# Meta queries of a latent attention layer: scores as masked rows instead of small column products

## The chip, the cores and the metric

The kernel runs on one core of one Trainium2 chip. The metric is the device time of one execution in microseconds (us); lower is better. All arithmetic is fp32; the large products are made of three products each, of operands split into a rounded upper part (`_hi`) and a rest (`_lo`).

## The reference

Two transformer blocks of two layers each, 1024 wide, over 256 tokens; in the first block 16 meta tokens stand in front of them (272 positions, `T`). The change lies in the second layer of the first block, a latent attention with 16 heads:

```python
s = (jnp.einsum('bqhd,bkhd->bhqk', qn, k_nope)
     + jnp.einsum('bqhr,bkr->bhqk', qr, k_rope)).astype(jnp.float32) * scale
p = jax.nn.softmax(jnp.where(mask, s, -jnp.inf), axis=-1)
return jnp.einsum('bhqk,bkhd->bqhd', p.astype(v.dtype), v)
```

A query sees keys of its own chunk of 64 positions and of earlier ones; the 16 meta positions are the first chunk, so that a meta query sees the 16 meta keys only. Each head's query and key are 96 wide (64 without position, 32 rotary). What follows this layer is a feed-forward net with a causal convolution over three positions, and after it only the 256 real tokens count. So of the meta positions only the last two (14 and 15) are carried through this attention: 258 columns of queries instead of 272.

## The kernel before

The kernel is one program with an instruction list per engine: TensorE (PE) multiplies, VectorE (DVE) and ScalarE (ACT) move results out of PSUM, split weights into their two parts and do the softmax, GpSimd (POOL) does sums of squares and small copies, SyncE loads weights. Engines wait on semaphores. The order of the work is written out by hand.

The latent stage is `latent_stage` on each engine. PE goes over 32 weight blocks (step `s`, `latent_block`), and between them come the steps of eight pairs of heads `n`, at the steps given by `SCORES_AT["B"]`, `TURN_AT["B"]` and `MIX_AT["B"]`; steps over 31 lie between the first pieces of the output projection. For a pair:

- `latent_scores` (PE): for both heads `e` the scores of two query tiles of 128 against 144 and 272 keys (L1025). An fp32 product is two records in the trace.
- `latent_maxima` (DVE): four operations (L2271) that add the mask, write `S` and give the smallest value of the negated scores, then the bias for the exponential (`nb`, L2277).
- `latent_probs` (ACT): four exponentials (L1683). `latent_norm` (DVE): one over the sums, then four scalings (L2298).
- `latent_turn` (PE): the probabilities are transposed (L1037, L1041), after `normed`. `latent_pt` (ACT) copies them to `PT`.
- `latent_mix` (PE): the product with the values (L1055), after `b_meta_placed`.

The scores go to one of three banks, `score_bank(n, e)`; `maxed` counts the maxima and frees the banks.

The two meta queries of four heads are handled together, with the odd pair `n` of each two (group `b = n // 2`, four groups). In `latent_scores` there are four products (L1019, eight records) with 16 meta keys stationary and two query columns moving, which give keys down the rows and 8 columns. DVE negates and copies them (L2266), then after `nb` transposes a 32x32 block (L2283), takes the minimum (L2285) and makes the bias (L2287). ACT takes one exponential of 8x16 after the pair's four (L1688). `latent_norm` ends with the reciprocal (L2303), the scaling (L2306) and the transposition back (L2308). POOL then copies 16x8 into `PT` (L2725) and signals `b_meta_placed`, for which `latent_mix` of both pairs of the group waits. The semaphore `meta_dve` counts DVE's steps.

Two pieces run once: at step 1 DVE clears two tiles of 32x128 (L2154, L2155) after two rests of the latent products (L2231) and ahead of the split of the next weights (`refill`, L1956); at step 6 it lays out the meta positions' scale factors (`fm`, L2191), which PE transposes (L1000) and ACT stores as `rq`.

## Time and profile before

| | |
|---|---|
| median of 3 runs | 1211.8 us (1211.45 to 1211.91) |
| the profiled execution's own time | 1211.74 us |
| its span in the trace | 1209.9 us |
| latent stage's scores, turns and mixes | about 362 to 423 us of the span |
| PE clock granted | 1.00 throughout |

The span runs from the first to the last instruction in the trace; the execution's own time has 1.8 us more around it. The engines overlap, so that a busy time is no share of the end by itself. In a timeline each row has its start, the time from its start to the end of the last of its group, the engine, the line, the operation, output and inputs, and the count; idle time of the engine before it and what ended it stand in brackets. Matmuls overlap one another in the record, so what one costs is the distance from its start to the next one's.

### The profile page before, as it was taken

What the parts mean: (1) busy time and instruction counts of PE and PEld (TensorE: products, weight loads), DVE (VectorE), ACT (ScalarE), POOL (GpSimd) and SP (SyncE); (2) the same over time, 40 slices, a digit from 0 to 9 for tenths busy, and PEclk for the clock granted to TensorE, in tenths of its full rate; (3) what the DMA queues carried; (4) which work ended last, traced back from release to release, by engine and by line L of the source; (5) the groups of instructions that cost most, each with busy time, mean ns of one, the idle gap of its engine ahead of it and who ended that gap; (6) DMA issues with size and microseconds to landing.
All of it is one profiled execution on the core that took longest, in us unless ns stands there. A gap on an engine that the chain in (4) does not pass through costs nothing.

```text
span 1209.9 us, 26142 instructions
## 1 busy us (share of the span) xinstructions
PE 1202.5 (99%) x9943; PEld 1170.7 (97%) x9943; DVE 883.0 (73%) x1720; ACT 698.2 (58%) x1371; POOL 165.9 (14%) x176
## 2 busy tenths in 40 slices
PE   9999999999999999999999999999999999999998
PEld 8999999999998899999999999999999999999998
DVE  6988777776778878777668987666656877767443
ACT  6776555554468755554448855564336785556332
POOL 1111500002330040000670032000210003100000
PEclk9999999999999999999999999999999999999999
DMA  9333444435543245554566345455553334455451
GB/s 347 122 140 113 165 178 173 173 120 192 205 165 105 79 154 188 186 184 144 189 229 239 117 148 201 175 196 187 176 196 129 132 134 175 175 194 189 177 192 49
DMA packets 32237, 203.71 MB, mean 168 GB/s; under 512 B 3584, under 2 KB 4608, under 8 KB 11792
## 3 DMA queue, kind: packets, MB, share of 16 engines
q1 hardware_dynamic: 31248, 198.95, 45.9%
q0 software_dynamic: 896, 3.49, 0.8%
q8 instruction: 62, 1.02, 0.3%
q14 instruction: 31, 0.25, 0.1%
HBM read 201.10 MB, written 1.05 MB: 167 GB/s over the span
## 4 chain that ended last, share of the span: by engine, by line
PE 94%; DVE 4%; ACT 1%; issue 1%; DMA 0%; SPq 0%; ACTq 0%; DVEq 0%
PE ps L801 28%; PE ps L802 28%; PE ps L803 28%; DVE w_lo L1956 1%; PE ps L1209 1%; PE ps L902 1%; PE ps L903 1%; PE ps L904 1%; PE ps L1194 1%; PE ps L1180 1%; PE ps L1296 1%; PE ps L1055 1%; PE ps L1025 0%; DVE E_S L2411 0%; DMA raw<-in_weights 0%
## 5 line engine op out<-in xcount | busy, mean ns | idle before, releaser
L1956 DVE TENSOR_TENSOR w_lo<-raw,w_hi 128x1024 fp32r<-128x1024 f32 (+2 forms) x391 | 463.2, 1218 | 94.8 <-ACT w_hi L1429 93.9
L1429 ACT ACTIVATE w_hi<-raw 128x1024 fp32r<-128x1024 f32 (+2 forms) x391 | 376.0, 1002 | 188.9 <-PE ps L803 186.2
L801 PE MATMUL ps<-x_hi,w_hi 128*128 128x256 f32 (+2 forms) x1384 | 396.7, 287 | 0.1
L802 PE MATMUL ps<-x_lo,w_hi 128*128 128x256 f32 (+2 forms) x1384 | 392.0, 283 | 0.0
L803 PE MATMUL ps<-x_hi,w_lo 128*128 128x256 f32 (+2 forms) x1384 | 391.3, 283 | 0.0
L801 PEld LDWEIGHTS ps<-x_hi,w_hi 128*128 128x128 f32 x1384 | 260.6, 188 | 3.3 <-issue 1.6
L802 PEld LDWEIGHTS ps<-x_lo,w_hi 128*128 128x128 f32 x1384 | 260.3, 188 | 0.4
L803 PEld LDWEIGHTS ps<-x_hi,w_lo 128*128 128x128 f32 x1384 | 260.3, 188 | 0.0
L801 PE MATMUL ps<-X_x_hi,w_hi 128*128 128x256 f32 (+2 forms) x568 | 161.6, 285 | 0.0
L802 PE MATMUL ps<-X_x_lo,w_hi 128*128 128x256 f32 (+2 forms) x568 | 160.1, 282 | 0.0
L803 PE MATMUL ps<-X_x_hi,w_lo 128*128 128x256 f32 (+2 forms) x568 | 159.3, 281 | 0.0
L801 PE MATMUL ps<-G_g_hi,w_hi 128*128 128x256 f32 x512 | 143.8, 281 | 0.0
L802 PE MATMUL ps<-G_g_lo,w_hi 128*128 128x256 f32 x512 | 143.8, 281 | 0.0
L803 PE MATMUL ps<-G_g_hi,w_lo 128*128 128x256 f32 x512 | 143.8, 281 | 0.0
L801 PEld LDWEIGHTS ps<-X_x_hi,w_hi 128*128 128x128 f32 x568 | 106.8, 188 | 0.6 <-issue 0.5
L803 PEld LDWEIGHTS ps<-X_x_hi,w_lo 128*128 128x128 f32 x568 | 107.0, 188 | 0.0
L802 PEld LDWEIGHTS ps<-X_x_lo,w_hi 128*128 128x128 f32 x568 | 106.8, 188 | 0.1
L803 PE MATMUL ps<-F_g_hi,w_lo 128*128 128x272 f32 (+1 forms) x352 | 100.3, 285 | 0.0
L801 PE MATMUL ps<-F_g_hi,w_hi 128*128 128x272 f32 (+1 forms) x352 | 100.2, 285 | 0.0
L802 PE MATMUL ps<-F_g_lo,w_hi 128*128 128x272 f32 (+1 forms) x352 | 99.9, 284 | 0.0
L802 PEld LDWEIGHTS ps<-G_g_lo,w_hi 128*128 128x128 f32 x512 | 96.6, 189 | 0.0
L803 PEld LDWEIGHTS ps<-G_g_hi,w_lo 128*128 128x128 f32 x512 | 96.6, 189 | 0.0
(337 smaller groups left out, 1818.0 us busy)
## 6 DMA issues: line engine op xcount, KB each, us to landing
raw<-in_weights SPq DMA_DIRECT2D x159, 1024.0 KB, 4.8
raw<-in_weights SPq DMA_DIRECT2D x32, 704.0 KB, 4.1
raw<-in_weights SPq DMA_DIRECT2D x4, 832.0 KB, 4.4
E_bias<-in_even_bias POOLq DMA_DIRECT2D x4, 768.0 KB, 8.8
raw<-in_weights SPq DMA_DIRECT2D x6, 256.0 KB, 6.8
out<-h SPq DMA_DIRECT2D x8, 128.0 KB, 4.8
h<-in_tokens SPq DMA_DIRECT2D x3, 272.0 KB, 6.5
cst<-in_consts SPq DMA_DIRECT2D x1, 808.0 KB, 11.0
```

What stands on the lines that cost most here:

```text
L801: pe.matmul(target, hi, xs[0], start=start, stop=False)
L802: pe.matmul(target, hi, xs[1], start=False, stop=False)
L803: return pe.matmul(target, lo, xs[0], start=False, stop=stop)
L902: pe.matmul(to, x[0], w_hi[:, at + w0:at + w1], start=c == 0, stop=False)
L903: pe.matmul(to, x[0], w_lo[:, at + w0:at + w1], start=False, stop=False)
L904: mm = pe.matmul(to, x[1], w_hi[:, at + w0:at + w1], start=False, stop=c == KC - 1)
L1055: mm = pe.matmul(bank(7, to, cols, slice(64 * e, 64 * e + 64)), oB[v][0:keys, f:f + 64], oB["PT"][0:keys, at:at + cols], start=k == 0, sto ...
L1180: mm = pe.matmul(bank(3 + e, col, nk), a.o["qk"][p, q + t * P:q + t * P + P], a.o["qk"][p, k:k + nk], start=a.name == "E", stop=a.name == ...
L1194: tr = pe.transpose(bank(5 + e, b * P, P), a.o["S"][:, at + b * P:at + b * P + P], c_("ident", 0, P))
L1209: mm = pe.matmul(bank(7, n % 2 * SEQ + lo, cols, slice(64 * e, 64 * e + 64)), a.o["V"][:, vc:vc + 64], a.o["PT"][:, at:at + cols], start=k ...
L1429: act.activation(w_hi[:, to + a:to + b], raw[:, fr + a:fr + b], ACT.Copy).then_inc(hi_made, 1)
L1956: dve.tensor_tensor(w_lo[:, to + a:to + b], raw[:, fr + a:fr + b], w_hi[:, to + a:to + b].bitcast(F32), ALU.subtract).then_inc(lo_made, 1)
```

## The change

For a group of four heads the products are made the other way round. The four heads' queries at one meta position `c` are stationary (four columns, one from each head), and the 16 meta keys of all four heads move past them (64 columns). Two products, `c` = 0 and 1, write rows 0 to 3 and rows 32 to 35 of the bank. Of the 64 columns a row needs the 16 of its own head; a mask `mm` puts the rest out of play. DVE adds mask and negated scores and takes the minimum in one operation per `c`; ACT's exponential covers 64 rows by 64 columns; the scaled result goes to `mN` with 32 columns per head, is transposed as 64x128, and POOL places it with two copies, one per `c`. The factors `fm` are laid out for 64 rows. `meta_dve` counts four steps a group instead of six.

```diff
-                     ("rk", 8, F32), ("rq", 4, F32), ("nb", 32, F32), ("mS", P, F32), ("mT", P, F32), ("mP", P, F32),
-                     ("PTq", P, F32), ("mx", 16, F32), ("PT", 4 * B_TURNED, F32))
+                     ("rk", 8, F32), ("rq", 4, F32), ("nb", 32, F32), ("mT", 256, F32), ("mP", 256, F32), ("mN", 512, F32), ("mm", 64, F32),
+                     ("PTq", 528, F32), ("mx", 16, F32), ("PT", 4 * B_TURNED, F32))
...
+        def four_heads(name, n):
+
+            at = (n - 1) % 4 * 2 * T
+            return oB[name][:, at:at + 4 * T].rearrange("p (h t) -> p h t", h=4)
...
-                tr = pe.transpose(bank(6, 80, 16, slice(0, 32)), oB["fm"][0:16, 0:32], ident)
+                tr = pe.transpose(bank(6, 80, 16, slice(0, 64)), oB["fm"][0:16, :], ident)
...
-                    for e in range(2):
-                        for i in range(2):
-                            pe.matmul(bank(score_bank(n, 0), 416 + 4 * e + 2 * i, 2, slice(0, META)), stacked("K", n - 1 + i, e, 0, META),
-                                      stacked("Q", n - 1 + i, e, META - 2, 2), start=True, stop=True)
+                    keys, queries = four_heads("K", n), four_heads("Q", n)
+                    for c in range(2):
+                        pe.matmul(bank(score_bank(n, 0), 416, 64, slice(32 * c, 32 * c + 4)), queries[:, :, META - 2 + c],
+                                  keys[:, :, 0:META], start=True, stop=True)
...
-                    act.wait_ge(meta_dve, 1 + 6 * b + 3)
-                    act.activation(oB["mP"][0:8, 32 * b:32 * b + META], oB["mT"][0:8, 32 * b:32 * b + META], ACT.Exp,
+                    act.wait_ge(meta_dve, 1 + 4 * b + 1)
+                    act.activation(oB["mP"][0:64, 64 * b:64 * b + 64], oB["mT"][0:64, 64 * b:64 * b + 64], ACT.Exp,
...
-                        dve.memset(oB["mS"][0:32, :], 0.0)
-                        dve.memset(oB["mP"][0:32, :], 0.0).then_inc(meta_dve, 1)
+                        dve.memset(oB["mT"][0:64, :], 0.0)
+                        dve.memset(oB["mN"][0:64, :], 0.0)
+                        dve.memset(oB["mx"][0:64, :], 0.0)
+                        for c in range(2):
+                            rows, own = slice(32 * c, 32 * c + 32), CST["ident"] + 32 * c
+                            op = dve.tensor_scalar(oB["mm"][rows, :].rearrange("p (h k) -> p h k", h=4),
+                                                   cst[rows, own:own + 4].unsqueeze(2).broadcast_to([32, 4, META]), -NEG, NEG, ALU.mult, ALU.add)
+                        op.then_inc(meta_dve, 1)
...
-                    dve.tensor_scalar(oB["mS"][0:META, 32 * b:32 * b + 8], bank(score_bank(n, 0), 416, 8, slice(0, META)), -1.0, None, ALU.mult)\
-                       .then_inc(meta_scored, 1)
+                    for c in range(2):
+                        rows = slice(32 * c, 32 * c + 4)
+                        op = dve.tensor_tensor_reduce(oB["mT"][rows, 64 * b:64 * b + 64], bank(score_bank(n, 0), 416, 64, rows), oB["mm"][rows, :],
+                                                      -1.0, BIG, ALU.add, ALU.min, oB["mx"][rows, 4 * b:4 * b + 1])
+                    op.then_inc(meta_scored, 1)
...
-                    dve.transpose(oB["mT"][0:32, 32 * b:32 * b + 32], oB["mS"][0:32, 32 * b:32 * b + 32]).then_inc(meta_dve, 1)
-                    dve.wait_ge(meta_dve, 1 + 6 * b + 1)
-                    dve.tensor_reduce(oB["mx"][0:8, 4 * b:4 * b + 1], oB["mT"][0:8, 32 * b:32 * b + META], AX.X, ALU.min).then_inc(meta_dve, 1)
-                    dve.wait_ge(meta_dve, 1 + 6 * b + 2)
-                    dve.scalar_tensor_tensor(oB["mx"][0:8, 4 * b + 1:4 * b + 2], oB["mx"][0:8, 4 * b:4 * b + 1], -1.0, oB["rq"][0:8, 2:3],
+                    dve.scalar_tensor_tensor(oB["mx"][0:64, 4 * b + 1:4 * b + 2], oB["mx"][0:64, 4 * b:4 * b + 1], -1.0, oB["rq"][0:64, 2:3],
...
-                    part = oB["mP"][0:8, 32 * b:32 * b + META]
-                    dve.tensor_scalar(part, part, oB["mx"][0:8, 4 * b + 3:4 * b + 4], None, ALU.mult).then_inc(meta_dve, 1)
-                    dve.wait_ge(meta_dve, 1 + 6 * b + 5)
-                    dve.transpose(oB["PTq"][0:32, 32 * b:32 * b + 32], oB["mP"][0:32, 32 * b:32 * b + 32]).then_inc(meta_dve, 1)
+                    dve.tensor_scalar(oB["mN"][0:64, P * b:P * b + P].rearrange("p (h k) -> p h k", h=4)[:, :, 0:META],
+                                      oB["mP"][0:64, 64 * b:64 * b + 64].rearrange("p (h k) -> p h k", h=4),
+                                      oB["mx"][0:64, 4 * b + 3:4 * b + 4], None, ALU.mult).then_inc(meta_dve, 1)
+                    dve.wait_ge(meta_dve, 1 + 4 * b + 3)
+                    dve.transpose(oB["PTq"][0:64, P * b:P * b + P], oB["mN"][0:64, P * b:P * b + P]).then_inc(meta_dve, 1)
...
-                pool.tensor_copy(oB["PT"][0:META, :].rearrange("p (n e c) -> p n e c", n=2, e=2)[:, :, :, 0:2],
-                                 oB["PTq"][0:META, 32 * b:32 * b + 8].rearrange("p (e n c) -> p n e c", n=2, e=2)).then_inc(b_meta_placed, 1)
+                for c in range(2):
+                    own = oB["PTq"][32 * c:32 * c + META, P * b:P * b + 4 * 33].rearrange("p (h r) -> p h r", h=4)
+                    op = pool.tensor_copy(oB["PT"][0:META, :].rearrange("p (h r) -> p h r", h=4)[:, :, c:c + 1], own[:, :, 0:1])
+                op.then_inc(b_meta_placed, 1)
```

## Rows read from the trace of the kernel before

**Rows 1.** The page: busy time, share of the span and instructions of each engine.
```profile
PE 1202.5 (99%) x9943; PEld 1170.7 (97%) x9943; DVE 883.0 (73%) x1720; ACT 698.2 (58%) x1371; POOL 165.9 (14%) x176
```

**Rows 2.** Timeline of PE where scores of pairs 2 and 3 begin.
```profile
378.42 0.29 PE L803 MATMUL ps<-B_c_hi,w_lo 128*128 128x258 f32 x1
378.54 1.57 PE L1025 MATMUL ps<-B_K,B_Q 128*128 128x144 f32 x8
...
381.65 0.28 PE L803 MATMUL ps<-B_c_hi,w_lo 128*128 128x258 f32 x1
381.86 0.35 PE L1019 MATMUL ps<-B_Q,B_K 128*16 128x2 f32 x8
382.14 1.67 PE L1025 MATMUL ps<-B_K,B_Q 128*128 128x144 f32 x8
```

**Rows 3.** Timeline of PE at the end of pair 0's mix.
```profile
377.15 0.28 PE L1055 MATMUL ps<-B_PT,B_Vm 80*64 80x64 f32 x4
377.36 0.38 PE L801 MATMUL ps<-B_c_hi,w_hi 128*128 128x258 f32 x1
```

**Rows 4.** Timeline of PE where the turns of pairs 0, 3 and 4 begin.
```profile
369.51 0.39 PE L978 MATMUL ps<-w_lo,B_c_hi 128*128 128x512 f32 x1
369.75 0.40 PE L979 MATMUL ps<-w_hi,B_c_lo 128*128 128x512 f32 x1
370.17 0.39 PE L1037 MATMUL ps<-cst,B_S 128*16 128x128 f32 x2
...
392.66 0.39 PE L1037 MATMUL ps<-cst,B_S 128*16 128x128 f32 x2 [0.89 <-DVE B_S L2298]
...
399.39 0.28 PE L1037 MATMUL ps<-cst,B_S 128*16 128x128 f32 x1 [0.21 <-DVE B_S L2298]
```

**Rows 5.** Timeline of DVE in the maxima of pair 1, group 0.
```profile
366.01 0.16 DVE L2266 TENSOR_SCALAR B_mS<-ps 16x8 f32<-16x8 f32 x1 [0.40 <-PE ps L1025]
...
366.09 0.28 DVE L2271 CUSTOM_DVE_ANT_0 B_S<-ps,cst 128x144 f32<-128x144 f32 x1
...
366.32 0.42 DVE L2271 CUSTOM_DVE_ANT_0 B_S<-ps,cst 128x272 f32<-128x272 f32 x1
...
366.68 0.29 DVE L2271 CUSTOM_DVE_ANT_0 B_S<-ps,cst 128x144 f32<-128x144 f32 x1
...
367.45 0.19 DVE L2283 STREAM_TRANSPOSE B_mT<-B_mS 32x32 f32<-32x32 f32 x1
...
367.87 0.15 DVE L2287 SCALAR_TENSOR_TENSOR B_mx<-B_mx,B_rq 8x1 f32<-8x1 f32 x1
```

**Rows 6.** Timeline of DVE where pair 3's norm begins.
```profile
391.34 0.18 DVE L2293 RECIPROCAL rden<-den 128x4 f32<-128x4 f32 x1 [0.73 <-ACT B_S L1683]
```

**Rows 7.** Timeline of DVE and PE at step 1 of the latent stage.
```profile
342.65 0.17 DVE L2154 MEMSET B_mS<- 32x128 f32 x1
...
343.13 1.23 DVE L1956 TENSOR_TENSOR w_lo<-raw,w_hi 128x1024 fp32r<-128x1024 f32 x1 [0.18 <-ACT w_hi L1429]
...
345.68 0.48 PE L801 MATMUL ps<-x_hi,w_hi 128*128 128x258 f32 x1
...
349.72 0.49 DVE L2231 SCALAR_TENSOR_TENSOR B_c_lo<-ps,vec,B_c_hi 128x258 fp32r<-128x258 f32 x1 [1.55 <-ACT B_c_hi L1629]
```

**Rows 8.** Timelines of POOL, DVE and PE around the placing of groups 1 to 3.
```profile
393.21 0.18 POOL L2725 COPY B_PT<-B_PTq 16x8 f32<-16x8 f32 x1 [20.32 <-DVE B_PTq L2308]
...
393.85 0.44 PE L1055 MATMUL ps<-B_PT,B_V 128*64 128x258 f32 x2
...
407.87 1.17 DVE L1956 TENSOR_TENSOR w_lo<-raw,w_hi 128x1024 fp32r<-128x1024 f32 x1
...
407.99 1.09 POOL L2725 COPY B_PT<-B_PTq 16x8 f32<-16x8 f32 x1 [14.60 <-DVE B_PTq L2308]
...
418.82 2.36 DVE L1956 TENSOR_TENSOR w_lo<-raw,w_hi 128x1024 fp32r<-128x1024 f32 x2 [0.25 <-ACT w_hi L1429]
...
420.05 0.44 PE L1055 MATMUL ps<-B_PT,B_V 128*64 128x258 f32 x2
```

More of the change, by code:

```diff
@@ L282, in program @@
         oB = overlay("B_", ("K", 8 * T, F32), ("Q", 8 * T, F32), ("kr", T, F32), ("V", 2 * D, F32),
-                     ("Vm", D, F32), ("c_hi", 5 * T, F32R), ("c_lo", 5 * T, F32R), ("sq", 5 * T, F32), ("fm", 32, F32),
+                     ("Vm", D, F32), ("c_hi", 5 * T, F32R), ("c_lo", 5 * T, F32R), ("sq", 5 * T, F32), ("fm", 64, F32),
                      ("S", 4 * 416, F32),
@@ L1686, in latent_probs @@
                     b = n // 2
-                    act.wait_ge(meta_dve, 1 + 6 * b + 3)
-                    act.activation(oB["mP"][0:8, 32 * b:32 * b + META], oB["mT"][0:8, 32 * b:32 * b + META], ACT.Exp,
-                                   scale=oB["rq"][0:8, 2:3], bias=oB["mx"][0:8, 4 * b + 1:4 * b + 2],
-                                   accum_out=oB["mx"][0:8, 4 * b + 2:4 * b + 3]).then_inc(meta_exped, 1)
+                    act.wait_ge(meta_dve, 1 + 4 * b + 1)
+                    act.activation(oB["mP"][0:64, 64 * b:64 * b + 64], oB["mT"][0:64, 64 * b:64 * b + 64], ACT.Exp,
+                                   scale=oB["rq"][0:64, 2:3], bias=oB["mx"][0:64, 4 * b + 1:4 * b + 2],
+                                   accum_out=oB["mx"][0:64, 4 * b + 2:4 * b + 3]).then_inc(meta_exped, 1)
             def refill(st, s):
@@ L2190, in latent_stage @@
                             dve.wait_ge(f_made, 3)
-                            dve.tensor_copy(oB["fm"][0:16, :].rearrange("p (d t) -> p d t", t=2),
-                                            f[0:16, META - 2:META].unsqueeze(1).broadcast_to([16, 16, 2])).then_inc(f_made, 1)
+                            dve.tensor_copy(oB["fm"][0:16, :].rearrange("p (t d) -> p t d", t=2),
+                                            f[0:16, META - 2:META].unsqueeze(2).broadcast_to([16, 2, 32])).then_inc(f_made, 1)
                     if s == KR_AT:
@@ L2302, in latent_norm @@
                     dve.wait_ge(meta_exped, b + 1)
-                    dve.reciprocal(oB["mx"][0:8, 4 * b + 3:4 * b + 4], oB["mx"][0:8, 4 * b + 2:4 * b + 3]).then_inc(meta_dve, 1)
-                    dve.wait_ge(meta_dve, 1 + 6 * b + 4)
-                    part = oB["mP"][0:8, 32 * b:32 * b + META]
-                    dve.tensor_scalar(part, part, oB["mx"][0:8, 4 * b + 3:4 * b + 4], None, ALU.mult).then_inc(meta_dve, 1)
-                    dve.wait_ge(meta_dve, 1 + 6 * b + 5)
-                    dve.transpose(oB["PTq"][0:32, 32 * b:32 * b + 32], oB["mP"][0:32, 32 * b:32 * b + 32]).then_inc(meta_dve, 1)
+                    dve.reciprocal(oB["mx"][0:64, 4 * b + 3:4 * b + 4], oB["mx"][0:64, 4 * b + 2:4 * b + 3]).then_inc(meta_dve, 1)
+                    dve.wait_ge(meta_dve, 1 + 4 * b + 2)
+                    dve.tensor_scalar(oB["mN"][0:64, P * b:P * b + P].rearrange("p (h k) -> p h k", h=4)[:, :, 0:META],
[3 more added lines that the diff above has]
+                    dve.transpose(oB["PTq"][0:64, P * b:P * b + P], oB["mN"][0:64, P * b:P * b + P]).then_inc(meta_dve, 1)
             def refill(st, s):
@@ L2719, in _ @@
             for b in range(PAIRS // 2):
-                pool.wait_ge(meta_dve, 1 + 6 * (b + 1))
+                pool.wait_ge(meta_dve, 1 + 4 * (b + 1))
                 if b:
```

## The prediction

> **What bounds the kernel now.** I read the page first: TensorE is busy for 99% of the span, and no other engine for more than 73% [rows 1]. So the end moves only by what PE itself does more or less of, and by what it is made to wait. I then read PE's timeline and its waits over the latent stage, because the change lies there alone. The reader is to see two things. PE's own price of the meta products is the distance from the last weight product to the pair's scores, with and without them [rows 2]. And PE does wait in this stage: before the turns of pairs 0, 3 and 4 it stands idle for DVE's scaled probabilities [rows 4]. So DVE's timeline counts too, at those places and nowhere else; I read it where the meta work stands ahead of a thing that PE waits for [rows 5, 6], at the stage's start [rows 7], and POOL's where the mix waits for its copy [rows 8].
>
> **PE's part.** With no meta products, pair 2's scores follow the last weight product by 378.54 - 378.42 = 0.12 us. With them, pair 3's follow by 382.14 - 381.65 = 0.49 us, and the first eight score records take 1.67 instead of 1.57 us, so 0.10 more is lost in the change back to wide products [rows 2]. A group's meta products thus cost 0.37 + 0.10 = 0.47 us, 1.9 us over four groups. Inside, eight records take 0.35 us to the end of the last. The step in takes 381.86 - 381.65 = 0.21 us against 0.12; it stays, as the new products are narrow too (4 of 128 columns of the array).
>
> The new group has four records with 64 moving columns, two for rows 0 to 3 and two for rows 32 to 35. The nearest rows are the last products of a mix: four records of 64 columns, each pair of them in another half of the array's columns. They reach from 377.15 to the next weight product at 377.36, 0.21 us in all, the change back included [rows 3]. In the new group I take these 0.21 us, the 0.21 us in, and 0.04 us for a first record that starts late: 0.46 against 0.49 us, 0.03 us less. That supposes that the two products run side by side as the two halves do. If they do not, each of the four records has its own place: the four together end after 0.28 us and one of them lasts some 0.22, so that two places take 0.06 us; twice that is 0.12 us, and the group costs 0.06 to 0.09 us more than before. If 64 columns cost no more than 2, four places of 0.025 us go (eight records in 0.35 us, of which the last one lasts some 0.17, make 0.025 a place [rows 2]), and the group costs some 0.07 to 0.10 less. I take 0.03 less, because rows 3 have the same number of columns and the same kind of neighbours; the ends are 0.09 more and 0.10 less.
>
> The Trainium skill, TensorE: Matmul & The Clock Gate, section Back-to-back issue gap, gives a floor of about 25 ns between two starts and lets everything from 1 to 64 columns cost the same. For the two-column records the trace agrees (0.025 us). By the rule the swap from 2 to 64 columns would be free and the group would save 0.10 us; for an fp32 record of 64 columns the trace shows 0.06 us, and I go by that. By the rule my sum would be lower by 0.14 us, for two groups.
>
> Of four groups two count. In groups 1 and 2 the meta products stand ahead of a turn at which PE waits anyway (turn 3's chain starts in DVE; turn 4 waits too [rows 4]), and what they save or cost is taken up by that wait. Groups 0 and 3 count: 2 x -0.03 = -0.06 us.
>
> **DVE's part, ahead of the maxima.** The negating copy went, from 366.01 to the next start at 366.09, 0.08 us; two masked minima of 4x64 come, of the kind of L2271, with their accumulator reads. Start to start that kind takes 0.23 us at 144 columns and 0.36 us at 272, so 0.001 us a column [rows 5]; at 64 columns 0.15 us, two of them 0.30. So the maxima and `nb` of an odd pair come 0.22 us later. The ends: 0.08 us each, as the copy, gives 0.08 more; 0.23 each, as at 144 columns, 0.38 more.
>
> **DVE's part, after `nb`.** Transposition and minimum go: 367.87 - 367.45 = 0.42 us [rows 5]. So DVE is 0.22 us later at `nb` and 0.20 us earlier after it.
>
> **Where that meets PE.** Turn 0: DVE works without a gap from group 0's maxima to pair 0's scaling, so pair 0's probabilities come 0.20 us earlier. PE's place between its last two weight products is 369.75 - 369.51 = 0.24 us and the turn begins 0.42 us after the last of them, so that it waits 0.18 us [rows 4]. That wait goes: -0.18 us.
>
> Turn 3: here `nb` of pair 3 starts the exponentials, and DVE then waits for ACT for 0.73 us before it can scale [rows 6]; what it saved after `nb` falls into that wait. The chain maxima, `nb`, exponentials, scaling, turn is late by the whole 0.22 us, and PE, idle for 0.89 us there, waits 0.22 us longer [rows 4].
>
> Turn 4: behind pair 3's scaling stand the reciprocal, the wider scaling (64x64 in place of 8x16, 48 columns more) and the transposition of 64x128 in place of 32x32, then pair 4's maxima, a weight split and pair 4's scaling, with no gap. No row has a wide transposition. By the 0.001 us a column of rows 5 the two grow by 0.05 and 0.10 us, together 0.15. The ends are nothing and, with four times the 0.19 us of L2283 [rows 5] for four times the columns, 0.6 us. I take 0.15, as every wide DVE operation in these rows grows by about that slope. PE waits there (0.21 us shown [rows 4]), so +0.15 us.
>
> After turn 4 PE's turns do not wait. The single exponential on ACT grows by 48 columns. I cost it at nothing, because it stands after the pair's four exponentials and DVE's scaling of the pair needs only those; ahead of them, at the slope of 0.001 us a column, it would cost 0.05 us.
>
> **At the start.** DVE's two clearings take (343.13 - 0.18 - 342.65) = 0.30 us [rows 7]. In their place come clearings of 64x256, 64x512 and 64x16 and two small masks. A start-to-start of 0.15 us at 128 columns gives at most 0.0012 us a column, so at most 0.3 + 0.6 + 0.15 (the small one) and 0.15 each for the masks, 1.35 us; with the 0.001 slope it is about 1.1. DVE gets 0.8 to 1.05 us later, less the 0.18 it had waited for ACT. Behind them is queued the split L1956 of 1.23 us: it ended at 344.36, and PE first needs those weights at 345.68, a cover of 1.3 us against 0.9 at most. By 349.72 DVE waits 1.55 us for ACT, and the lateness is gone [rows 7]. Cost: nothing. Without that cover up to 0.9 us. The wider `fm` adds 32 rows to one small transposition and 0.03 us to one DVE copy, once, in the same gap.
>
> **POOL.** One copy becomes two of 16x4, with no new wait. They lie between DVE's transposition and the mix. The tightest is group 1: the copy starts at 393.21 and takes 0.18, the mix starts at 393.85, 0.46 us after its end [rows 8]. Two copies of 0.18 that start 0.37 us later (0.22 + 0.15) end at 393.94, and PE reaches its mix at 393.85 + 0.22 - 0.18 - 0.03 = 393.86 at the earliest; 0.1 us at most, and then turn 4's wait takes it up. Cost: nothing.
>
> **The sum.** -0.06 - 0.18 + 0.22 + 0.15 = +0.13 us. Against the profiled execution's own 1211.74 us that is 1211.87; it stands 0.06 us under the median of 1211.8, so the forecast is 1211.9 us. That cannot be told from no change: 0.2%, 2.4 us, is about what a measurement of this kernel can tell.
>
> **The rivals.**
>
> *The two copies wait behind DVE (slower).* Group 2's copy takes 1.09 us instead of 0.18: it began 0.12 us after a split L1956 of 1.17 us and ended with it [rows 8]. If every copy of a group cost 1.09 us, group 1's two would end at 393.21 + 0.37 + 2.18 = 395.76, 1.9 us after PE's 393.86; group 2's, at 407.99, would add up to 0.6 and group 3's another 0.5: 1211.9 + 3.0 = 1214.9 us. It decides once the two take over 0.5 us in group 1. Against it: group 1's copy took 0.18 us, with the maxima on DVE at the same time; these read PSUM and one tile in SBUF, the split reads two. The Trainium skill, SBUF — State Buffer, section Who interferes with whom, has that rule: a DVE instruction with two SBUF inputs keeps out a GpSimd instruction that reads SBUF. The trace agrees, 1.09 against 0.18. Chance 5%.
>
> *Only the last group is caught.* The last group's second copy, now behind a wider transposition, comes close to the start of two splits in a row at 418.82, which last 2.36 us to 421.18; the mix that needs it starts at 420.05 [rows 8]. If the copy waits for both, PE stands 1.3 us: 1213.2 us. If it slips between the two, nothing. For it: the splits wait for ACT and do not move with DVE. Chance 12%.
>
> *The start is not covered.* Price up to 0.9 us: 1212.8 us. Against it: the cover of 1.3 us. Chance 8%.
>
> *The products do not run side by side, or the wide transposition takes 0.8 us.* +0.24 and +0.45 us: 1212.1 to 1212.6 us. Chance 20%.
>
> *DVE is relieved rather than burdened.* The minima cost 0.08 more and the transposition nothing more, and the products 0.10 less each: -0.20 - 0.18 + 0.08 = -0.30, 1211.4 us. Chance 15%. To be faster by 2.4 us, all four groups' 1.9 us and turn 0's wait would have to go and more; 2% for what I do not see.
>
> **How the numbers follow.** 38% for the forecast as it stands (within 0.3 us), 20% and 15% for its neighbours on either side, 8% and 12% for the two that reach 1212.8 and 1213.2, 5% for the slower one, 2% for faster. The range goes from 1210.9 (1211.4 less half a microsecond, which is the spread of the three runs) to 1213.4 (the last group caught, and a little). Same within 0.2% (1209.4 to 1214.2): 93%; slower 5%; faster 2%.
>
> **What would show it.** In the changed profile: the meta products as four records per group, with about 0.46 us from the last weight product to the scores (0.55 to 0.6 if not side by side); 0.15 us from one 4x64 minimum to the next; turn 0 at its weight product's heels with 0.24 us; the wait before turn 3 at about 1.1 us instead of 0.89; two copies of about 0.18 us on POOL, one of group 2's at about 1.1; no wait of PE for `w_lo` between 343 and 350 us. The prediction is wrong if PE waits for POOL before a mix, if it waits for weights at 345.7, or if a 4x64 minimum has a fixed cost of half a microsecond, since that would come in twice before turn 3 and hold ACT's exponentials up in every group.

## The result, and the profile after

The changed kernel takes 1214.63 us, the median of 13 runs (1213.78 to 1216.63), beside 1211.68 us of the kernel before in as many (1211.2 to 1212.98): a ratio of 1.0024, interval 1.0017 to 1.0032. It is 2.95 us slower. The forecast was 1211.9 us with a range to 1213.4; the time lies 1.2 us above the range and just beyond the 0.2% that a measurement can tell. The profiled execution took 1216.42 us of its own, with a span of 1214.4 us, the second highest of the 13; the last fence of this section shows why, and a second profile of the same kernel (the tenth run) lacks that.

The page, where the shares stand as they stood in [rows 1]:

```profile
PE 1203.5 (99%) x9927; PEld 1171.1 (96%) x9927; DVE 883.9 (73%) x1727; ACT 698.2 (57%) x1371; POOL 170.0 (14%) x180
```

PE has 16 instructions less, DVE 7 more and POOL 4 more, with 4.1 us more of busy time on POOL. No share moves by more than the last digit shown, and only POOL's time hints at what happened.

PE's timeline at the scores of pair 3, as in [rows 2]:

```profile
382.07 0.28 PE L808 MATMUL ps<-B_c_hi,w_lo 128*128 128x258 f32 x1
382.28 0.28 PE L1024 MATMUL ps<-B_K,B_Q 128*4 128x64 f32 x4
382.49 1.45 PE L1030 MATMUL ps<-B_K,B_Q 128*128 128x144 f32 x7
```

Four records in 0.28 us, so the two products do run side by side, and the scores follow the last weight product by 0.42 us (before 0.49).

PE at the turns of pairs 0, 3 and 4 and at mix 2, as in [rows 4] and [rows 8]:

```profile
370.04 0.40 PE L984 MATMUL ps<-w_hi,B_c_lo 128*128 128x512 f32 x1
370.45 0.60 PE L1042 MATMUL ps<-cst,B_S 128*16 128x128 f32 x4
...
393.36 0.60 PE L1042 MATMUL ps<-cst,B_S 128*16 128x128 f32 x4 [1.21 <-DVE B_S L2308]
...
394.72 0.66 PE L1060 MATMUL ps<-B_PT,B_V 128*64 128x258 f32 x4
...
400.23 0.50 PE L1042 MATMUL ps<-cst,B_S 128*16 128x128 f32 x3 [0.25 <-DVE B_S L2308]
```

Turn 0 still follows its weight product by 0.41 us; turn 3 waits 1.21 us instead of 0.89.

DVE at the minima of group 0, as in [rows 5]:

```profile
366.28 0.21 DVE L2279 CUSTOM_DVE_ANT_0 B_mT<-ps,B_mm 4x64 f32<-4x64 f32 x1 [0.32 <-PE ps L1030]
...
366.51 0.22 DVE L2279 CUSTOM_DVE_ANT_0 B_mT<-ps,B_mm 4x64 f32<-4x64 f32 x1
...
366.77 0.31 DVE L2285 CUSTOM_DVE_ANT_0 B_S<-ps,cst 128x144 f32<-128x144 f32 x1
```

The two take 366.77 - 366.28 = 0.49 us, where the forecast had 0.30. What they replace did not take 0.08 us everywhere either. That figure is group 0's; in group 1, whose turn is the one that PE waits for, the negating copy of the kernel before took 387.53 - 387.34 = 0.19 us:

```profile
387.34 0.15 DVE L2266 TENSOR_SCALAR B_mS<-ps 16x8 f32<-16x8 f32 x1
387.53 0.31 DVE L2271 CUSTOM_DVE_ANT_0 B_S<-ps,cst 128x144 f32<-128x144 f32 x1
```

POOL's four placings, and the last one taken apart, as in [rows 8]:

```profile
373.13 0.41 POOL L2738 COPY B_PT<-B_PTq 16x4 f32<-16x4 f32 x2 [16.40 <-DVE B_PTq L2319]
394.05 0.41 POOL L2738 COPY B_PT<-B_PTq 16x4 f32<-16x4 f32 x2 [20.52 <-DVE B_PTq L2319]
408.86 1.32 POOL L2738 COPY B_PT<-B_PTq 16x4 f32<-16x4 f32 x2 [14.39 <-DVE B_PTq L2319]
...
419.86 2.56 POOL L2738 COPY B_PT<-B_PTq 16x4 f32<-16x4 f32 x1 [9.69 <-DVE B_PTq L2319]
422.46 0.18 POOL L2738 COPY B_PT<-B_PTq 16x4 f32<-16x4 f32 x1
```

DVE beside it, and PE at mix 6:

```profile
419.50 0.30 DVE L2319 STREAM_TRANSPOSE B_PTq<-B_mN 64x128 f32<-64x128 f32 x1
419.73 0.38 DVE L2220 TENSOR_TENSOR x_lo<-ps,x_hi 128x258 fp32r<-128x258 f32 x1
420.04 2.33 DVE L1961 TENSOR_TENSOR w_lo<-raw,w_hi 128x1024 fp32r<-128x1024 f32 x2
```

```profile
422.90 0.98 PE L1060 MATMUL ps<-B_PT,B_V 128*64 128x258 f32 x8 [1.79 <-POOL B_PT L2738]
...
423.93 0.43 PE L806 MATMUL ps<-x_hi,w_hi 128*128 128x258 f32 x1
424.16 0.42 PE L807 MATMUL ps<-x_lo,w_hi 128*128 128x258 f32 x1
```

This is the loss. The last group's first copy, 0.18 us of work, begins at 419.86 and ends at 422.42, with the second of the two splits (420.04 + 2.33 = 422.37). The second copy ends at 422.46 + 0.18 = 422.64, and PE, which stood ready 1.79 us earlier, begins mix 6 at 422.90. At that place PE is 1.86 us later than before; nothing else comes near.

Laid side by side, PE's matmul starts in the two traces of the changed kernel differ from those of before by steps at these places (worked out as the start after less the start before, each the change of that difference):

| place in the stage | forecast | first profile | second profile (tenth run) |
|---|---|---|---|
| products of groups 0, 1, 2 | -0.03, 0, 0 | -0.06, -0.05, -0.07 | -0.07, -0.07, -0.09 |
| turn 0 | -0.18 | 0.00 | 0.00 |
| weight products at 371.4 | 0 | +0.12 | +0.12 |
| turn 3 | +0.22 | +0.31 | +0.30 |
| mix 2 | 0 | +0.17 | +0.16 |
| turn 4 | +0.15 | +0.04 | +0.06 |
| scores of pair 7, with group 3's products | -0.03 | +0.15 | +0.15 |
| mix 6 | 0 | +1.86 | +1.86 |
| whole stage | +0.13 | +2.5 | +2.5 |

The forecast's +0.15 at turn 4 was meant from turn 3 on, with mix 2's lateness taken up by the wait there. Between the starts of turns 3 and 4 the difference grows by 0.14 us in both profiles (0.70 to 0.84, and -0.06 to 0.08), mix 2's +0.17 included.

The first profile has 1.5 us more, right behind mix 6. Windows of it over PE, with PEclk the granted clock as a share of 2.4 GHz:

```profile
422.90:424.00 1.10, 1.10 (x13) 0.94 (x13) 0.00 (x0) 0.00 (x0) 0.00 (x0) 1.00 0.55 82
424.00:425.00 1.00, 1.00 (x5) 1.00 (x6) 0.43 (x1) 0.39 (x1) 0.00 (x0) 0.56 0.71 246
425.00:426.00 1.00, 1.00 (x7) 1.00 (x6) 0.00 (x0) 0.00 (x0) 0.00 (x0) 0.50 1.02 434
426.00:428.00 2.00, 2.00 (x16) 1.35 (x15) 0.00 (x0) 0.00 (x0) 0.00 (x0) 0.62 0.36 147
```

PE had stood idle for 1.79 us and worked again at 1.00 until just after 424.0; then the clock fell to 0.50, the level of 1.2 GHz, and was back at 1.00 before 428. The weight products last 0.42 us there instead of the 0.28 of L808 above. Two of the 13 executions have a mean clock of 0.999 instead of 1.000, and they are the two of 1216.4 and 1216.6 us.

### The profile page after: what moved, and what is told of

The parts are those of the page before. It is cut to its first block, busy times and chain, and to the rows that moved or that the text cites. A ratio compares the mean times of both kernels' runs of the same rounds, so it can differ in the third digit from the quotient of the medians.

```text
span 1214.4 us, 26121 instructions
## 1 busy us (share of the span) xinstructions
PE 1203.5 (99%) x9927; PEld 1171.1 (96%) x9927; DVE 883.9 (73%) x1727; ACT 698.2 (57%) x1371; POOL 170.0 (14%) x180
## 4 chain that ended last, share of the span: by engine, by line
PE 90%; DVE 6%; ACT 1%; issue 1%; DMA 1%; POOL 0%; SPq 0%; ACTq 0%; DVEq 0%
PE ps L806 27%; PE ps L807 27%; PE ps L808 27%; DVE w_lo L1961 1%; PE ps L1214 1%; PE ps L907 1%; PE ps L908 1%; PE ps L909 1%; PE ps L1199 1%; PE ps L1185 1%; DVE B_S L2285 1%; PE ps L1301 1%; DMA raw<-in_weights 1%; DVE B_S L2308 0%; ACT B_S L1688 0%
## 5 line engine op out<-in xcount | busy, mean ns | idle before, releaser
L808 PE MATMUL ps<-x_hi,w_lo 128*128 128x256 f32 (+2 forms) x1384 | 391.9, 283 | 0.0
L808 PEld LDWEIGHTS ps<-x_hi,w_lo 128*128 128x128 f32 x1384 | 260.9, 188 | 0.0
L808 PE MATMUL ps<-X_x_hi,w_lo 128*128 128x256 f32 (+2 forms) x568 | 159.3, 281 | 0.0
L808 PE MATMUL ps<-G_g_hi,w_lo 128*128 128x256 f32 x512 | 143.8, 281 | 0.0
L808 PEld LDWEIGHTS ps<-X_x_hi,w_lo 128*128 128x128 f32 x568 | 107.0, 188 | 0.0
L808 PE MATMUL ps<-F_g_hi,w_lo 128*128 128x272 f32 (+1 forms) x352 | 100.4, 285 | 0.0
L808 PEld LDWEIGHTS ps<-G_g_hi,w_lo 128*128 128x128 f32 x512 | 96.6, 189 | 0.0
```

Of the source, the lines that this page charges most:

```text
L808: return pe.matmul(target, lo, xs[0], start=False, stop=stop)
```

## The experiments

The theory after the first trace: the two small minima, dearer than thought and ahead of `nb`, make DVE late; the last group's copies then run into the two splits; that is 1.9 us, and the rest is a row of tenths.

**1. Two copies in the kernel before.** Does doubling POOL's copies cost anything where they are on time?

```diff
-                pool.tensor_copy(PT[0:META, all four heads, 0:2], PTq[0:META, 32 * b:32 * b + 8])
+                for c in range(2):
+                    op = pool.tensor_copy(PT[0:META, all four heads, c:c + 1], PTq[0:META, every other column from 32 * b + c])
```

(the views are shortened)

> The kernel before, with POOL's one copy per group made into two (one per meta position), all else as it was. Two theories. 'Port': the changed kernel's loss is the last group's second copy, which comes to the port after DVE has begun two weight splits in a row and waits for both. Here the first copy starts at 418.33 and the second would start by 418.55 and end by 418.75, just ahead of the splits at 418.82, so doubling alone costs nothing: 1211.7 us, within 0.3. 'Doubling': two copies cost the loss by themselves, wherever they stand: then this kernel shows the wait of 1.8 us before pair 6's mix and 1213.5 us.

Measured: 1211.76 us in 11 runs, ratio 1.0000 (0.9991 to 1.0009). The last group's copies:

```profile
418.27 0.30 POOL L2726 COPY B_PT<-B_PTq 16x4 f32<-16x4 f32 x2 [9.11 <-DVE B_PTq L2308]
```

They end at 418.57 and the first split begins at 418.77. The number of copies alone costs nothing, at the last group or at mix 2, which stands where it stood. These two are cheaper than those of the changed kernel, though: 0.30 us together against 0.41.

**2. The changed kernel, copies ahead of the splits.** DVE waits for the placing before the last group's two splits.

```diff
+                        dve.wait_ge(b_meta_placed, 4)
```

> The changed kernel; DVE waits for b_meta_placed of the last group before the two weight splits of the output projection's last slot. No operation is added or taken away, only the order of the last group's copies and those two splits is fixed. 'Port': the wait of 1.79 us before pair 6's mix goes, both copies take 0.4 us, time 1.8 us less than the changed kernel (1212.8 us). Rival 'late chain': the mix waits because DVE's meta work itself comes late by 0.5 us and more, and the order of the splits has no part in it: the wait stays over 1 us.

Measured: 1213.10 us (1212.63 to 1213.31), ratio 1.0010 (1.0001 to 1.0019). POOL and DVE:

```profile
419.90 0.41 POOL L2739 COPY B_PT<-B_PTq 16x4 f32<-16x4 f32 x2 [9.67 <-DVE B_PTq L2320]
```

```profile
420.34 1.23 DVE L1961 TENSOR_TENSOR w_lo<-raw,w_hi 128x1024 fp32r<-128x1024 f32 x1 [0.19 <-POOL B_PT L2739]
```

With 0.19 us of waiting on DVE, both copies take 0.41 us, PE's wait at mix 6 is gone, and the stage ends 0.7 us late instead of 2.5. The steps ahead of mix 6 are those of the table. By this edit alone the meeting of copies and splits is worth 1.5 us of the median (1.7 by each kernel's distance from the kernel before, measured beside it) and 1.86 us of the trace.

**3. The changed kernel, the last group's minima behind `nb`.** Are the minima what made the copies late?

```diff
-                    (both minima ahead of the maxima, in every group)
+                    if b < 3:
+                        meta_minima(n)
...
                     (nb)
+                    if b == 3:
+                        meta_minima(n)
```

> The changed kernel; in the last group alone the two 4x64 minima stand behind nb of pair 7 instead of ahead of the maxima. The sum of DVE's work is the same. If it is the 0.49 us of minima ahead of nb that make the last group's copies late (exponentials, then the split that DVE makes before pair 7's norm, then the norm), the copies start 0.3 to 0.5 us earlier against PE, before the two splits, and the wait before pair 6's mix falls from 1.79 us to 0.3 or less: 1.5 to 1.8 us less than the changed kernel, about 1213.0 us. Rival: the minima have no part in it (the wider scaling and transposition and the second copy, 0.4 us, are enough to miss the port): the wait stays at 1.3 us or more.

Measured: 1212.57 us (1211.92 to 1213.41), ratio 1.0006 (0.9997 to 1.0015). The copies:

```profile
419.14 0.41 POOL L2745 COPY B_PT<-B_PTq 16x4 f32<-16x4 f32 x2 [9.19 <-DVE B_PTq L2326]
```

The same work in another order brings the copies back ahead of the splits, which begin at 419.59 after a wait of 0.20 us for ACT. So the minima ahead of `nb` are what made the copies miss. They are not all of it: the copies end at 419.55, which leaves 0.04 us of the 0.31 that the kernel before had, so the second copy, the wider scaling and the wider transposition use up the rest. The minima's path goes through ACT. ACT before, then ACT after (the last pair's exponentials, then the weights of the split ahead of pair 7's norm, then those of the two last splits):

```profile
411.67 0.51 ACT L1683 ACTIVATE B_S<-B_S,B_nb,B_rq 128x144 f32<-128x144 f32 x1 [0.46 <-DVE B_nb L2277]
...
414.25 1.04 ACT L1429 ACTIVATE w_hi<-raw 128x1024 fp32r<-128x1024 f32 x1
...
417.74 2.00 ACT L1429 ACTIVATE w_hi<-raw 128x1024 fp32r<-128x1024 f32 x2
```

```profile
413.02 0.51 ACT L1688 ACTIVATE B_S<-B_S,B_nb,B_rq 128x144 f32<-128x144 f32 x1 [0.82 <-DVE B_nb L2291]
...
415.65 1.04 ACT L1434 ACTIVATE w_hi<-raw 128x1024 fp32r<-128x1024 f32 x1
...
418.73 2.00 ACT L1434 ACTIVATE w_hi<-raw 128x1024 fp32r<-128x1024 f32 x2
```

The exponentials are 1.35 us later, the first weight store 1.40 (0.05 of it the wider meta exponential), and with it DVE's split, the norm and the transposition; but the last stores are only 0.99 us later, as late as PE itself at that point. Before, the copy ended at 418.33 + 0.18 = 418.51, 0.31 us ahead of the split at 418.82. After, the first copy would end at 420.04 and the split begins at 420.04.

**4. One minimum over 64 rows.** The stationary operand takes 32 evenly spaced query columns, so that rows 0 to 63 are all written, and one masked minimum of 64x64 replaces two of 4x64; its mask is made a little otherwise, and two clearings go.

```diff
-                        pe.matmul(bank(score_bank(n, 0), 416, 64, slice(32 * c, 32 * c + 4)), queries[:, :, META - 2 + c],
+                        pe.matmul(bank(score_bank(n, 0), 416, 64, slice(32 * c, 32 * c + 32)), oB["Q"][:, at + c:at + c + 31 * 34 + 1:34],
...
-                    for c in range(2):
-                        rows = slice(32 * c, 32 * c + 4)
+                    for rows in (slice(0, 64),):
```

> The changed kernel; the stationary operand of each of the two products takes 32 evenly spaced columns instead of 4 (every eighth is a head's meta query, the others are queries that nobody reads), so that rows 0 to 63 are all written and ONE masked minimum over 64 rows takes the place of two over 4. The clearings of mT and mx go, mm is made from a sum over the identity. Expected: 0.24 us less DVE ahead of nb in each group, so the turn of pair 3 comes 0.24 us earlier, and turn 0 0.2 us earlier. In the last group the copies start 0.24 us earlier against PE (the first at 419.6 by the changed kernel's time, the second ends at 420.0, against splits at 420.04): a close race. If it is won, 2.2 us less than the changed kernel, 1212.4 us; if not, 0.4 less, 1214.2 us. If the products' price on PE grows with the 32 columns, the group shows it between the weight product and the scores (0.42 us in the changed kernel).

Measured: 1212.06 us (1211.74 to 1212.61), ratio 1.0002 (0.9993 to 1.0012). DVE at group 0, then PE at 371.4:

```profile
366.07 0.22 DVE L2278 CUSTOM_DVE_ANT_0 B_mT<-ps,B_mm 64x64 f32<-64x64 f32 x1 [0.40 <-PE ps L1030]
...
366.22 0.29 DVE L2284 CUSTOM_DVE_ANT_0 B_S<-ps,cst 128x144 f32<-128x144 f32 x1
```

```profile
371.52 0.37 PE L806 MATMUL ps<-B_c_hi,w_hi 128*128 128x272 f32 x1 [0.24 <-issue]
```

One minimum costs 0.15 us, as the forecast had it for each. Turn 3 is on time and so are the last copies. Turn 0 now gains 0.21 us, and 1.2 us later PE gives 0.25 us back. The trace names no releaser there ("issue"); what these products need at that place is the eviction L1664 of their bank by ACT, which stands behind pair 1's exponentials. They begin 0.10 to 0.11 us after its end in three traces: here, in the changed kernel (371.71, then 371.81) and in the kernel before (371.31, then 371.42). The products with 32 stationary columns cost as much as the eight small ones before.

**5. The same, copies ahead of the splits as well.** Is anything left in the meeting?

> The kernel with one minimum, and DVE waits for the last group's copies before the two splits, as in the run with the copies first. With one minimum the copies (0.41 us from 418.68) ended at 419.09 and the splits began at 419.05, so the race was won by the order in which they were issued. 'Port': making the order sure changes nothing, 1212.0 us, equal to one minimum alone within 0.3. If the runs of one minimum lost the race now and then, this one has fewer high times and a narrower spread.

Measured: 1211.92 us (1211.40 to 1212.67), ratio 1.0001 (0.9992 to 1.0010). Nothing that can be told from the fourth run.

**6. One minimum, behind `nb` in groups 0, 1 and 3.** PE gets a wait before it overwrites the bank.

```diff
+                        if n in (2, 4):
+                            pe.wait_ge(meta_scored, n // 2)
...
+                    if b == 2:
+                        meta_minimum(n)
...
                     (nb)
+                    if b != 2:
+                        meta_minimum(n)
```

> The kernel with one minimum, which stands after nb in groups 0, 1 and 3 (PE waits for it before it writes that bank again, for pairs 2 and 4). Nothing stands ahead of nb then, against the 0.08 to 0.19 us of the negating copy in the kernel before. Expected: 0.15 us off the turn of pair 3, and the mix of pair 2 that followed 0.12 us late; time 0.2 to 0.3 us less than one minimum alone: 1211.7 us, at or a little under the kernel before. Rival: those waits are not bound by nb any more and the time stays at 1212.0.

Measured: 1211.99 us (1211.56 to 1212.58), ratio 1.0001 (0.9992 to 1.0010). Turn 3 comes 0.19 us earlier than before, but by mix 2 0.15 of it is gone; turn 0 gains 0.17 and the products at 371.4 give back 0.21. The forecast of 1211.7 us was not reached.

**7. Two minima of 32 rows.** Is it the second operation that is dear, or its four rows? The fourth kernel with `for rows in (slice(0, 32), slice(32, 64))`.

> The kernel with one minimum, made as two again, over rows 0 to 31 and 32 to 63 (64 columns each). It asks why two 4x64 minima took 0.49 us to the next start where one 64x64 took 0.15. If it is the four rows that cost, two of 32 rows take about 0.30. If the cost lies in each further minimum of this size, whatever its rows, they take 0.49 again.

Measured: 1214.70 us, one execution. DVE at group 0, and POOL's copy:

```profile
366.57 0.21 DVE L2278 CUSTOM_DVE_ANT_0 B_mT<-ps,B_mm 32x64 f32<-32x64 f32 x1 [0.38 <-PE ps L1030]
...
366.81 0.22 DVE L2278 CUSTOM_DVE_ANT_0 B_mT<-ps,B_mm 32x64 f32<-32x64 f32 x1
...
367.07 0.31 DVE L2284 CUSTOM_DVE_ANT_0 B_S<-ps,cst 128x144 f32<-128x144 f32 x1
```

```profile
420.33 2.33 POOL L2737 COPY B_PT<-B_PTq 16x4 f32<-16x4 f32 x1
```

0.24 and 0.26 us again: two minima in a row cost 0.50, one costs 0.15, and the number of rows has no part in it. And the loss is back, 1.57 us at mix 6, from nothing but this one split of an operation. Here the first copy got through in 0.18 us and the second was held.

One difference is left that the run does not take away: the second minimum's rows start at 32, those of its neighbours at 0. The trace of the kernel before shows elsewhere what such a step costs. Its line 2371 makes four operations in a row, two on rows 32 to 63 and two on rows 96 to 127; the first three:

```profile
931.02 0.42 DVE L2371 SCALAR_TENSOR_TENSOR O_c<-ps,O_c 32x256 fp32r<-32x256 f32 x1 [0.83 <-ACT O_c L1720]
931.37 0.27 DVE L2371 SCALAR_TENSOR_TENSOR O_c<-ps,O_c 32x128 fp32r<-32x128 f32 x1
931.65 0.43 DVE L2371 SCALAR_TENSOR_TENSOR O_c<-ps,O_c 32x256 fp32r<-32x256 f32 x1
```

The second, on the same rows, begins 0.07 us before the record of the first ends; the third, on other rows, 0.01 us after the end of the second. The minima do the same: the one of 64 rows is followed 0.07 us before its end (366.22 against 366.29), while both of the pair are followed 0.02 to 0.04 us after theirs. So the dearer minima are likely the price of moving to other rows and back, some 0.1 us each time, and not of a second operation as such. No run made two minima on the same rows, so this is read from the traces and not tested.

**8. A late copy in the kernel before.** POOL clears 128x640 of a scratch tile ahead of the last copy, so that it begins as the first split does.

```diff
+                if b == 3:
+                    pool.memset(oB["sq"][:, 0:640], 0.0)
```

> The kernel before, with one addition: POOL clears 128x640 of an unused tile (about 0.65 us) between its wait and the last group's copy. The copy, which began at 418.33, comes at about 419.0, after the two splits have begun at 418.82. 'Port': it waits for both, to 421.2, and PE stands 1.2 to 1.4 us before pair 6's mix: 1213.1 us. Rival, lateness only costs its own length: the copy ends at 419.2, 0.85 us ahead of the mix at 420.05, and nothing changes: 1211.8 us.

Measured: 1212.19 us (1211.6 to 1212.8), ratio 1.0003 (0.9994 to 1.0012). POOL, then PE at mix 6:

```profile
418.41 0.64 POOL L2726 MEMSET B_sq<- 128x640 f32 x1 [9.24 <-DVE B_PTq L2308]
418.99 1.20 POOL L2727 COPY B_PT<-B_PTq 16x8 f32<-16x8 f32 x1
```

```profile
420.44 0.98 PE L1055 MATMUL ps<-B_PT,B_V 128*64 128x258 f32 x8 [0.24 <-POOL B_PT L2727]
```

The expectation of over a microsecond failed: one late copy is held by the first split only, ends at 420.19 and costs 0.3 us. Lateness alone is not the loss either.

**9. The second copy on DVE.** The sixth kernel, with the second position's column placed by DVE itself right behind the transposition.

```diff
+                    place_meta(dve, b, 1).then_inc(meta_dve, 1)
...
-                for c in range(2):
-                    (POOL places position c)
+                place_meta(pool, b, 0).then_inc(b_meta_placed, 1)
```

> The kernel of the sixth run (one minimum over 64 rows, behind nb in groups 0, 1 and 3), in which GpSimd places only the first meta position's column of exponentials, and VectorE places the second itself right after its transposition, so that at no group two GpSimd copies stand one after the other between the transposition and TensorE's mix. Theory (the shift at mix 2 is the second copy's time, and what the last group cost is two copies meeting two splits): mix 2's +0.15 us goes, the last group's copy is on time, and the time is 1211.85 us, 1211.5 to 1212.2, not to be told from the kernel before. Rival (the copy on VectorE delays the next tile's maxima and turn 4 by as much as it saves): mix 2 near 0 but turn 4 0.15 to 0.2 later than in the sixth run, 1212.0 us. If instead the shift at mix 2 stays at +0.15, the copies had no part in it, and it comes from the turn of the scores ahead of it.

Measured: 1212.04 us (1211.48 to 1212.66), ratio 1.0001 (0.9992 to 1.0010). Both halves came out: mix 2 loses 0.05 us instead of 0.15, so the second copy was the cause there; and turn 4, where the sixth kernel lost nothing, loses 0.29. DVE's copy, which now stands ahead of pair 4's maxima, takes 0.19 us of that. The rest is what mix 2 no longer loses: turn 4 waits for DVE, and from turn 3 to turn 4 the sixth kernel takes 0.13 us longer than the kernel before, with mix 2's 0.15 inside, and this one 0.33. The rival's sum was the right one.

**10. The changed kernel again**, with blank lines as its only edit.

> The changed kernel again with nothing edited but blank lines, for a second profile of it and a time beside the other kernel's on the same chip. Theory (the last group's placing copies meet the two two-input splits of VectorE, and one of them is held until both end): 1214.6 us, 1213.8 to 1215.4; at mix 6 TensorE again waits some 1.8 us, one of the two copies lasts 2.3 to 2.6 us against 0.18 of the other; if the granted clock stays at 1.00, the stage as a whole is 2.6 to 3.0 us later than in the kernel before, and what the first profile had above that was the fall of the clock alone. Rival (the place of the meeting is chance, a few tenths of a microsecond either way decide it): the wait at mix 6 is 0.3 to 1.2 us in this profile, and the times spread from 1212.6 to 1215.

Measured: 1214.42 us in 11 runs (1213.7 to 1216.37), ratio 1.0025 (1.0016 to 1.0034). POOL, then PE:

```profile
419.09 2.79 POOL L2735 COPY B_PT<-B_PTq 16x4 f32<-16x4 f32 x2 [9.68 <-DVE B_PTq L2316]
```

```profile
422.13 0.66 PE L1057 MATMUL ps<-B_PT,B_V 128*64 128x258 f32 x4 [1.76 <-POOL B_PT L2735]
```

The same wait, with the clock at 1.00 throughout, and the stage 2.5 us late, a little under the 2.6 expected. The loss is no accident of one execution. Again two executions, 1216.37 and 1216.23 us, have the lower mean clock.

**11. Two late copies in the kernel before**: the edits of 1 and 8 together. It completes a square: one or two copies, on time or late.

> The kernel before with both alterations at once: the last group's placing as two GpSimd copies, and the clearing of 128x640 ahead of them, so that the first starts as VectorE's first split does (some 0.07 us after it, as in the eighth run). It tells why a single copy was held by one split in the eighth run and one of two by both splits in the changed kernel. Theory (the pair matters: one of two small copies is held until both splits end): one copy lasts 2.2 to 2.4 us, TensorE's mix 6 starts at about 421.6 us instead of 420.05, and the time is 1213.2 to 1213.6 us. Rival (the moment matters, or what the split had waited for ahead of it: a copy that finds DVE just out of a wait is let in between the two): the first copy lasts 1.2 us and the second 0.18, mix 6 at 420.5 to 420.7, and the time is 1212.2 to 1212.5 us.

Measured: 1213.46 us (1212.7 to 1214.06), ratio 1.0015 (1.0005 to 1.0024). POOL, then PE:

```profile
419.15 1.20 POOL L2728 COPY B_PT<-B_PTq 16x4 f32<-16x4 f32 x1
...
420.29 1.19 POOL L2728 COPY B_PT<-B_PTq 16x4 f32<-16x4 f32 x1
```

```profile
421.74 0.62 PE L1055 MATMUL ps<-B_PT,B_V 128*64 128x258 f32 x3 [1.37 <-ACT B_PT L1672]
```

The time is the theory's, but neither theory had the pattern: each copy is held by one split. The first ends at 420.35 with the first split, the second begins at 420.29, after the second split's start, and ends at 421.48 with it. PE starts 0.26 us later; the profile puts its wait down to ACT, whose copy had long been done. Mix 6 is 1.44 us late. So in the kernel before: two copies on time, 0; one late, +0.3; two late, +1.44 us.

**12. The changed kernel, its copies 0.3 us later**, by a clearing of 128x320 on POOL ahead of them.

> The changed kernel with a clearing of 128x320 on GpSimd ahead of the last group's two copies, which start some 0.3 us later than in it, about 0.15 us into the first split instead of 0.18 us before it. Theory (the place inside the first split does not matter, a held copy is let go when both splits are through): the first copy lasts 2.2 to 2.3 us, the mix starts as late as in the changed kernel, and the time is 1214.5 us. Rival (the moment of the start matters): the first copy lasts 1.0 to 1.2 us and slips in between the splits, TensorE's wait at mix 6 is 0.5 to 1.0 us instead of 1.8, and the time is 1213.2 to 1213.8 us.

Measured: 1214.57 us in 8 runs (1213.82 to 1216.19), ratio 1.0026 (1.0015 to 1.0036). POOL:

```profile
419.42 0.37 POOL L2737 MEMSET B_sq<- 128x320 f32 x1 [9.68 <-DVE B_PTq L2319]
419.83 2.15 POOL L2740 COPY B_PT<-B_PTq 16x4 f32<-16x4 f32 x1
```

The copy now starts 0.23 us inside the first split and still ends with the second; mix 6 is 1.86 us late as before. The theory holds as far as it was tried: 0.04 us inside the first split (the seventh run's second copy, at 420.33 against 420.29) and 0.23 us inside it come to the same.

## Why the prediction was wrong

The step that failed is the treatment of the last group. The prediction costed the late `nb` at turn 3 and followed it no further, and put POOL's two copies at nothing; the runs show 1.86 us at mix 6, where those copies wait for DVE's two splits. That PE waits for POOL before a mix was the first of its own signs of being wrong. The rival "only the last group is caught" had the place and the mechanism, at 12% and 1.3 us. Three things were missing from it or wrong in it.

*The margin was not worked out.* The rival said that the splits wait for ACT and do not move with DVE. That is nearly so (their stores came 0.99 us later, the splits 1.22, behind DVE's own late work, and the copies 1.53), but it was left at "close". The argument of turn 3, that what DVE saves after `nb` falls into a wait while what it loses ahead of `nb` goes through ACT, holds for pair 7 word for word: its norm stands behind a split that waits for ACT, which waits for the exponentials. The prediction's own terms are 0.22 us at `nb`, 0.15 for the wider scaling and transposition and 0.18 for the second copy, 0.55 in all against a margin of 0.31: the meeting was the likelier case. The third run shows the path.

*The minima were mis-sized.* Two cost 0.49 us, not 0.30: start to start 0.23 and 0.26 where a single one costs 0.15 (fourth and seventh run). Against the negating copy that is 0.41 us more in group 0, but 0.30 in group 1, where the copy took 0.19 (the prediction had read group 0's 0.08 for all). Turn 3 moved by just that, +0.31 instead of +0.22. The term is also behind the lost margin.

*Its price.* 1.3 us was a single copy released at the end of the second split. Measured: the held copy ends 0.05 us after the split, the other takes 0.22 more, and PE begins 0.26 us after that: 1.86 us. The Trainium skill, SBUF — State Buffer, section Who interferes with whom, has the rule that a DVE instruction with two SBUF inputs contends with a GpSimd instruction that reads SBUF, and the traces agree throughout: 0.18 us alone, 1.20 and 1.19 us with a split each in the eleventh run, 2.56 with two. Of DVE's two-port modes the section also says that whoever issues first gets the shared pair for the whole instruction. Here a copy whose record begins 0.18 us ahead of the split was held all the same, and for two instructions, while in the seventh run one that begins 0.18 us ahead got through; the records do not tell the two apart.

The other terms:

- *Products.* Side by side as said, and cheaper by 0.06 to 0.09 us rather than 0.03. In group 3 the saving is covered by +0.15 at pair 7's scores.
- *Turn 0.* The 0.18 us did not come, because DVE's lateness and saving around `nb` nearly cancel once the minima cost 0.49. In the fourth run, where they come (0.21), ACT's queue takes them back 1.2 us later. In the kernel before, too, the products there began 0.11 us after ACT's eviction ended, so the gain was not to be had without moving ACT.
- *ACT at nothing.* The wider exponential and the late `nb` delay the eviction L1664: +0.12 us at 371.4.
- *Mix 2.* "0.1 at most, and then turn 4's wait takes it up": it was 0.17, the 0.25 us from the copy's end to PE's start being the part left out. The ninth run ties it to the second copy; the first run, whose two copies take 0.30 us instead of 0.41 and come at their old time, does not have it. It was taken up, as said: see turn 4.
- *Turn 4.* Right: +0.14 us from turn 3 to turn 4 against +0.15. The transposition of 64x128 takes 0.30 us in the record against 0.20 before, as estimated. The table shows only +0.04 at the turn itself because mix 2 had lost its part already.
- *Start.* DVE came to the first split about 1 us later and PE waited for nothing, as said.

Without the last group the stage is 0.66 us later, against +0.13 (-0.07 for group 0's products, +0.12 at 371.4, +0.31 at turn 3, +0.14 from there to turn 4, +0.15 at pair 7's scores); the last group adds 1.86, and together they give the stage's 2.5. The medians are 2.95 and 2.6 us apart; two executions in each set have the fall of the clock, and the first microseconds of the program vary by some tenths from trace to trace. Why one copy is held across both splits in the changed kernel and one by each in the kernel before is open. The traces that show the first (changed kernel, seventh, tenth and twelfth run) have no wait of DVE ahead of the splits, those that show the second (eighth and eleventh) have 0.25 us for ACT there; no run separates that from other differences. One of these is that the copies themselves differ: in the eighth and eleventh run they are those of the kernel before, which read their source in another layout. What pair 7's scores wait for, +0.15 us, was read only as ACT's late stores and not tested. No version beats the kernel before: the best, with one minimum, are at 1.0001 to 1.0002 with intervals across 1.

## What to carry to other kernels

A small operation on a slow engine that has a deadline against a long one elsewhere deserves a margin in the forecast: when it ends now, when the long one starts, and how much of either moves. Here a margin of 0.31 us met copies that came 0.5 us later against the stores that release the splits, and a second copy of 0.2 us; the answer was 1.9 us. Follow a delay ahead of a hand-over through every later use of the same chain, not only to the first stall that shows it; and when an operation is cut in two, price the pair from rows that have two in succession, on the rows of the tile where they will lie.

## What was not expected of the hardware

- Two small masked minima, the second on rows from 32 on, cost 0.23 and 0.26 us from start to start, whether of 4 or of 32 rows; one of 64 rows ahead of a wide one costs 0.15. In the kernel before, DVE operations of one line overlap by 0.07 us on the same rows and stand 0.01 us apart where the rows change (931.0 to 931.7 us).
- A GpSimd copy of 0.18 us was held through two successive two-input splits of DVE, 2.56, 2.33 and 2.15 us in three kernels, although 1.20 us and a release between the two occur as well.
- From the end of a copy on GpSimd to the start of the waiting matmul: 0.25 to 0.26 us (422.64 to 422.90, 421.48 to 421.74, 420.19 to 420.44).
- After 1.8 us without work for TensorE the granted clock fell in the first profile to 0.50, the level of 1.2 GHz, after 1.1 to 1.2 us of work at 1.00, at a price of 1.5 us. The mean clock is 0.999 in 5 of the 32 executions of the changed kernel and of the tenth and twelfth run, whose profiles have this wait (2 of 13, 2 of 11, 1 of 8), each at 1216.2 us or more; all the others are at 1.000 and at most 1215.2 us.
